# A recurrence on one core: the fourth head's decay levels move into the attention, a gate tile moves into the chunk steps, and the sample rows move ahead of a score block

## The chip, the cores and the metric

The kernel runs on one core of a Trainium2 chip. The metric is the device time of one launch in microseconds; of three timed runs before the change the median is 2238.07 us (2237.09 to 2239.33). Times inside the program are counted from the first instruction of one profiled execution. TensorE is called PE, VectorE DVE, ScalarE ACT, GpSimd POOL, and the engine that issues most transfers SP.

## The reference

One step of a decoder trunk of two layers, on 512 prompt tokens and 8 sequences of 8 sample tokens (576 columns in all). A layer projects its input, runs three mixers, merges them through sigmoid gates, and ends with a gated feed-forward block. The change lies in the second mixer, a gated recurrence with four heads:

```
def step(S, blk):                       # one chunk of one head
    qc, kc, vc, lc = blk
    L = jnp.cumsum(lc, axis=2)          # log decay since the chunk began
    inter = einsum('bhtk,bhkv->bhtv', qc * exp(L), S)
    diff = where(causal, L[:, :, :, None, :] - L[:, :, None, :, :], -inf)
    A = einsum('bhtk,bhsk,bhtsk->bhts', qc, kc, exp(diff))
    L_end = L[:, :, -1:, :]
    S = exp(L_end) * S + einsum('bhsk,bhsv->bhkv', kc * exp(L_end - L), vc)
    return S, inter + einsum('bhts,bhsv->bhtv', A, vc)
...
o_hg = rms_norm(o_hg) * silu(hgate)     # hgate: four 128-row tiles of x @ w_in
```

## The kernel before, in words

Every engine has an instruction order written out by hand; semaphores tie the engines together. In a layer come projections, the attention of the prompt (32 steps, a head and 128 queries each), the attention of the samples, the tiles of the pooling mixer and of `hgate`, the recurrence, the merge, the output projection and the feed-forward block.

The recurrence takes chunks of 128 tokens. A head has five steps: c = 0 to 3 for the prompt's chunks, c = 4 for the samples; step n of 20 is head n // 5, c = n % 5. exp(diff) is not formed per pair. A head has seven *levels* (block sizes 1 to 64): for each level a 512-column array holds log decays measured from the middle of a block (`level_differences`, L691 and L692), is put through exp by ACT (`decays_levels`, L1925), and its upper halves are multiplied by the queries (`level_scaled`, L700). The score block of a step is then many 32-column products on PE (`hg_pair_scores`, L1115 to L1124) and a transpose of the decayed keys (L1127). DVE masks and sums the score block (L2485, L2488, L2494); ACT copies the parts off the diagonal (`off_hg`, `hg_full`) and the transposed keys (`k_rows`), both at L1713. `hg_sums` on PE multiplies scores, state and values (L1152 to L1163), and DVE updates the state (L2516, L2518). In a sample step PE multiplies the eight sample states (the *sample rows*, L1173), makes the state updates (L1182) and the sample outputs (L1186, L1189); DVE copies the rows (`s_rows`, L2525) and updates the states (L2530).

The four heads have three level buffers; heads 0 and 3 share one. Head 2's levels are subtracted by POOL, head 3's too, at step 8 and after, when head 0's buffer is free. ACT makes head 3's exps in steps 10 and 11 (`LEVEL_STEPS`), DVE its products in steps 12 and 13 (`MULT_STEPS`).

Of `hgate`'s four tiles two are made whole on PE before the recurrence and put through silu by ACT. The other two are made inside it as four halves of 288 columns, one for each head, in pieces of 3, 3 and 2 matmuls (`gate_piece`, L1137) in the steps c = 1, 2, 3, between the next step's score block and this step's sums. ACT copies each half out of PSUM at c = 4 (`take_gate`) and applies silu in steps 13 and 19. PSUM bank 6 holds a half, and also sample state updates. exp and silu need different function tables on ACT; the table load before each change of function is an instruction of its own.

PE's loop over steps is:

```
for n in range(N_HG):
    if n + 1 < N_HG:
        hg_pair_scores(l, n + 1)
    h, c = divmod(n, N_CHUNK + 1)
    if 1 <= c < N_CHUNK:
        gate_piece(l, h, c - 1)
    hg_sums(l, n)
```

Of the kernel before, what the change touches and what calls it, by code (L numbers as in the profile page):

```python
# [71 lines left out]
LEV_BUF = (2, 0, 1, 2)  # L72
# [16 lines left out]
GATE_LOAD = MERGE0 - 1  # L89
# [54 lines left out]
TILE_YPOOL = TILE_HGATE + 2  # L144
# [21 lines left out]
def last_tiles():  # L166

    last = [TILE_CQ + 1, TILE_KPE, None, None, TILE_HQ + 1, TILE_HQ + 3, TILE_HI + 4, TILE_HI + 4]
    last += [TILE_U + 1, TILE_U + 3, TILE_HGATE + 1]
    assert len(last) == MERGE0 - 1  # L170
    return last
# [34 lines left out]
def build(nc, xT_in, w_stream, small_in, att_in, const_in, pages_in, kpe_in, page_table, pool_state,  # L206
          hgrn_state, conv_state, yT, ckv_out, kpe_out, pool_out, hgrn_p_out, hgrn_s_out, conv_out):
    with ExitStack() as ctx:
# [3 lines left out]
        def sem(name):  # L212
# [77 lines left out]
        lev_flat = [r1[:, 0:n_lev * SEQ], r1[:, n_lev * SEQ:2 * n_lev * SEQ], side[:, 4 * P + 2 * T:3 * HALF_DOWN]]  # L290
# [177 lines left out]
        def slot(tile):  # L468
            s = (tile + (TILE_U <= tile < TILE_YPOOL) + (TILE_YPOOL <= tile < TILE_SSQ_HG) + 3 * (tile >= TILE_SSQ_HG)) % 4
# [110 lines left out]
        gate_act = signal("gate_act", N_GATE + 2)  # L580
# [135 lines left out]
        def _(sp):  # L716
# [69 lines left out]
            with sp.Fori(0, DEPTH) as l:  # L786
# [53 lines left out]
                load(l, MERGE0)  # L840
# [65 lines left out]
        def _(pe):  # L906
# [222 lines left out]
            def gate_piece(l, h, x):  # L1129
                j, a = divmod(h, 2)  # L1130
                if h == 0 and x == 0:
                    pe.wait_ge(*w_ready[GATE_LOAD % 2].at(l, 16 * (GATE_LOAD // 2 + 1)))
                if h and x == 0:
                    pe.wait_ge(*hg_state.at(l, h * (N_CHUNK + 2)))
                w = w_tile(GATE_LOAD, j)
                for k in range(GATE_CHUNKS[x], GATE_CHUNKS[x + 1]):
                    mm = pe.matmul(bank[6][:, 0:HALF], w[k], xT[:, k, a * HALF:(a + 1) * HALF], start=(k == 0),  # L1137
                                   stop=(k == KD - 1))
                if x == 2:
                    mm.then_inc(gate_made.sem, 1)  # L1140

            def hg_sums(l, n):
# [22 lines left out]
                if h >= 1:  # L1165
                    pe.wait_ge(*hg_o_taken.at(l, 3 * h))
                    pe.wait_ge(*hg_sq.at(l, 2 * h))
                else:
                    pe.wait_ge(*state_s_ready.at(l, 16))
                for b in range(DEC_BATCH):  # L1170
                    x, j = divmod(b, S_PAIRS)
                    t0 = SEQ + min(DEC_SEQ * b, SAMPLES - SUB)
                    mm = pe.matmul(bank[5][SUB * j:SUB * (j + 1), 256 + x * P:256 + (x + 1) * P],  # L1173
                                   decayed[:, h % 2, 0, t0:t0 + SUB], state_s[:, b, h, :], start=True, stop=True)
                mm.then_inc(s_rows_made.sem, 1)
                pe.wait_ge(*gate_act.at(l, h + 1 + (h >= 2)))
# [351 lines left out]
            with pe.Fori(0, DEPTH) as l:  # L1528
# [170 lines left out]
        def _(act):  # L1699
# [94 lines left out]
            with act.Fori(0, DEPTH) as l:  # L1794
# [66 lines left out]
                for x in range(2):  # L1861
                    for lo, e in ((64, 0), (0, 1)):
                        rows = slice(lo, lo + 64)
                        copy(k96[rows, 2 * x:2 * x + 2, e, :], kpe[rows, 0:SEQ].unsqueeze(1).broadcast_to([64, 2, SEQ]),
                             scale=row_mask[rows, x:x + 1]).then_inc(k_rope.sem, 1)
                att_softmax(l, 0)
                for n in range(1, N_ATT + 2):
# [50 lines left out]
                def decays_levels(h, first, end):  # L1918
                    if first == 0:
                        act.wait_ge(*lev_diff.at(l, 2 * h + 1))  # L1920
                    b = LEV_BUF[h]
                    groups = [(first, end)] if b < 2 or end <= n_lev - 2 else [(v, v + 1) for v in range(first, end)]
                    for lo, hi in groups:
                        ap = lev_flat[b][:, lo * SEQ:hi * SEQ] if b < 2 or hi <= n_lev - 2 else level[b][lo]
                        ins = act.activation(ap, ap, ACT.Exp)  # L1925
                    if end == n_lev:
                        for ap in lev_s_flat[b]:
                            ins = act.activation(ap, ap, ACT.Exp)
                    if end == n_lev:
                        ins.then_inc(lev_exp.sem, 1)  # L1930
# [22 lines left out]
                for i, g in enumerate(GROUP_OF):  # L1953
                    act.wait_ge(*tile_ready.at(l, TILE_U + i + 1))
# [5 lines left out]
                decays_levels(1, 0, n_lev)  # L1960
                decays_ends(1)
                for j in range(2):
                    act.wait_ge(*tile_ready.at(l, TILE_HGATE + j + 1))
                    copy(two(hg_gate[:, j, :]), halves(TILE_HGATE + j), ACT.Silu).then_inc(tile_act.sem, 1)
# [10 lines left out]
                def gate_silu(j):  # L1975
                    act.wait_ge(*gate_act.at(l, (2, 5)[j - 2]))
                    act.activation(hg_gate[:, j, :], hg_gate[:, j, :], ACT.Silu).then_inc(gate_act.sem, 1)

                for n in range(N_HG):
# [22 lines left out]
                    if n == 13:  # L2002
                        gate_silu(2)
# [75 lines left out]
        def _(dve):  # L2079
# [173 lines left out]
            with dve.Fori(0, DEPTH) as l:  # L2253
# [170 lines left out]
                def ready_head(h):  # L2424
                    dve.wait_ge(*lev_exp.at(l, h + 1))
# [6 lines left out]
                dve.wait_ge(*log_k_ready.at(l, 1))  # L2432
                for h in range(2):
# [70 lines left out]
                def update(n):  # L2504
# [34 lines left out]
                for n in range(N_HG + 1):  # L2539
                    if n < N_HG:  # L2540
# [241 lines left out]
        def _(pool):  # L2782
# [146 lines left out]
            with pool.Fori(0, DEPTH) as l:  # L2929
# [26 lines left out]
                pool.tensor_tensor(log_k, log_k, logf, ALU.subtract).then_inc(log_k_ready.sem, 1)  # L2956

# [13 lines left out]
                differences(l, 3)  # L2971
# [311 lines left out]
```

## Time and profile before

| | |
|---|---|
| median of three timed runs | 2238.07 us |
| the profiled execution | 2238.98 us |
| its span, first to last instruction | 2237.2 us |
| mean granted clock of PE, as a share of 2.4 GHz | 0.993 |
| PE / DVE / POOL / ACT busy | 98% / 54% / 46% / 24% |

PE is busy nearly all the time; the other engines have room on average. The average hides single stretches in which another engine holds PE up; they are seen in the views of one stretch. A matmul of 32-bit floats stands in the trace as two records, so a gate piece of three matmuls reads x6. The recurrence of the first layer lies at 283 to 348 us, that of the second at 1392 to 1458 us.

### The profile page before, as it was taken

The page shows a single profiled execution, that of the slowest core. Times are in us where ns is not written, and L with a number is a line of the kernel's source. Part 1 is how long each engine was busy: PE and PEld are TensorE (multiplying, and loading weights), DVE is VectorE, ACT ScalarE, POOL GpSimd, SP SyncE. Part 2 cuts the span into 40 slices and gives each one's busy share as a digit, 9 for nine tenths or more (in the row PEclk, how much of TensorE's full clock was granted, in tenths as well). Part 3 has the DMA queues.
Part 4 walks back from the last instruction along what each step waited for, and adds up shares of the span by engine and source line. Part 5 has one row for each costly group of instructions (what it writes and reads, how often), then busy time and mean ns, then how long its engine had stood idle before and what let it go on. Part 6 is the DMA issues. An engine that isn't in the chain of part 4 may idle for free.

```text
span 2237.2 us, 37087 instructions
## 1 busy us (share of the span) xinstructions
PE 2189.7 (98%) x11824; PEld 1685.5 (75%) x11824; DVE 1202.1 (54%) x2152; ACT 525.9 (24%) x1112; POOL 1036.1 (46%) x1152
## 2 busy tenths in 40 slices
PE   8999999999999999999899999999999999999996
PEld 6776777777777777777676767777777777777775
DVE  2654675333577666661236447653336776666513
ACT  1453353111131111100134533521111411111002
POOL 3000146566656666633330002565767466665251
PEclk9999999999999999999999999999999999999998
DMA  5322113222132222122132221142211322222211
GB/s 210 106 74 78 43 64 134 67 85 85 57 108 77 85 82 75 69 74 77 39 135 88 75 68 66 41 144 81 79 68 57 127 75 75 75 78 79 86 52 42
DMA packets 51616, 183.54 MB, mean 82 GB/s; under 512 B 7234, under 2 KB 27970, under 8 KB 37762
## 3 DMA queue, kind: packets, MB, share of 16 engines
q1 hardware_dynamic: 50882, 178.49, 23.3%
q10 hardware_dynamic: 576, 3.06, 0.3%
q8 instruction: 84, 1.38, 0.3%
q14 instruction: 74, 0.61, 0.1%
HBM read 172.35 MB, written 9.18 MB: 81 GB/s over the span
## 4 chain that ended last, share of the span: by engine, by line
PE 93%; DVE 2%; issue 1%; POOL 1%; ACT 1%; SPq 1%; DMA 1%; DVEq 0%; ACTq 0%
PE ps L1315 25%; PE ps L1197 24%; PE ps L1357 17%; PE ps L917 9%; PE ps L986 3%; PE ps L949 2%; PE ps L1523 1%; PE ps L1387 1%; PE ps L1137 1%; PE ps L970 1%; PE ps L958 1%; PE ps L938 1%; PE ps L1038 1%; PE ps L1001 1%; PE ps L950 1%
## 5 line engine op out<-in xcount | busy, mean ns | idle before, releaser
L1315 PE MATMUL ps<-lq,mreg 128*128 128x288 f32 x1008 | 251.3, 406 | 0.0
L1315 PEld LDWEIGHTS ps<-lq,mreg 128*128 128x128 f32 x1008 | 191.5, 190 | 52.9
L1713 ACT ACTIVATE r<-ps 128x288 f32<-128x288 f32 (+7 forms) x264 | 112.9, 432 | 499.8 <-PE ps L1197 256.4
L1315 PE MATMUL ps<-xT,wring 128*128 128x288 f32 x672 | 169.8, 406 | 0.0
L917 PE MATMUL ps<-xT,wring 128*128 128x288 f32 (+2 forms) x640 | 156.2, 406 | 0.0
L1315 PEld LDWEIGHTS ps<-xT,wring 128*128 128x128 f32 x672 | 127.7, 190 | 35.3
L917 PEld LDWEIGHTS ps<-xT,wring 128*128 128x128 f32 x640 | 121.6, 190 | 33.7
L1197 PE MATMUL ps<-r,kbuf 128*128 128x288 f32 x576 | 143.6, 406 | 0.0
L1197 PEld LDWEIGHTS ps<-r,kbuf 128*128 128x128 f32 x576 | 109.4, 190 | 30.2
L2044 ACT ACTIVATE r<-r 128x592 f32<-128x592 f32 x44 | 30.7, 697 | 427.9 <-DVE r L2716 427.9
L2906 POOL TENSOR_TENSOR kbuf<-o_mla 128x288 f32<-128x288 f32 x42 | 33.4, 794 | 205.9 <-DVE o_mla L2680 205.9
L1713 ACT ACTIVATE o_mla<-ps 128x288 f32<-128x288 f32 (+1 forms) x108 | 45.2, 421 | 327.8 <-PE ps L1357 214.5
L2805 POOL TENSOR_TENSOR mreg<-vbuf,const 64x512 f32<-64x512 f32 x8 | 8.4, 1049 | 241.4 <-PE ps L1629 228.9
L1197 PE MATMUL ps<-xT,wring 128*128 128x288 f32 x448 | 113.4, 406 | 0.2 <-DMA wring<-w_stream 0.2
L2716 DVE SCALAR_TENSOR_TENSOR r<-r,small 128x592 f32<-128x592 f32 x88 | 106.3, 1209 | 12.4 <-DVE r L2713 12.1
L2713 DVE SCALAR_TENSOR_TENSOR r<-r,small 128x592 f32<-128x592 f32 x88 | 104.5, 1188 | 12.4 <-DVE r L2710 10.9
L1197 PEld LDWEIGHTS ps<-xT,wring 128*128 128x128 f32 x448 | 85.0, 190 | 24.5 <-issue 1.2
L1357 PE MATMUL ps<-r,side 128*128 128x288 f32 x372 | 92.7, 407 | 0.8 <-DVE r L2727 0.8
L1315 PE MATMUL ps<-xT,mreg 128*128 128x288 f32 x336 | 88.3, 406 | 0.0
L1315 PE MATMUL ps<-lq,wring 128*128 128x288 f32 x336 | 88.3, 406 | 0.0
L1197 PE MATMUL ps<-lq,r 128*128 128x288 f32 x336 | 87.4, 406 | 0.0
L1357 PEld LDWEIGHTS ps<-r,side 128*128 128x128 f32 x372 | 70.5, 190 | 21.0 <-issue 1.7
(459 smaller groups left out, 4659.4 us busy)
## 6 DMA issues: line engine op xcount, KB each, us to landing
wring<-w_stream SPq DMA_DIRECT2D x100, 1024.0 KB, 4.9
side<-w_stream SPq DMA_DIRECT2D x18, 704.0 KB, 4.5
r<-pages_in SPq DMA_DIRECT2D x80, 128.0 KB, 2.2
vbuf<-w_stream SPq DMA_DIRECT2D x12, 512.0 KB, 3.8
r<-w_stream SPq DMA_DIRECT2D x12, 512.0 KB, 3.6
wring<-w_stream SPq DMA_DIRECT2D x8, 704.0 KB, 4.1
r<-w_stream SPq DMA_DIRECT2D x6, 704.0 KB, 4.1
mreg<-pages_in SPq DMA_DIRECT2D x32, 128.0 KB, 2.1
```

What stands on the lines that cost most here:

```text
L917: mm = pe.matmul(out[0:w.shape[-1], a * 512:a * 512 + hi - lo], w, x[:, lo:hi], start=(k == 0), stop=(k == len(pairs) - 1))
L938: mm = pe.matmul(slot(tile + j)[:, a * 512:a * 512 + hi - lo], w, xT[:, k, lo:hi], start=(k == 0), stop=(k == KD - 1))
L949: pe.matmul(att_bank(n)[:, 0:keys], q96[:, j, e, t0:t0 + P], k96[:, j, e, 0:keys], start=True, stop=False)
L986: mm = pe.matmul(value_bank[g:g + rows, part * 256:(part + 1) * 256], xT[:, k, m * P:m * P + rows], w_slot[part][:, k * 256:(k + 1) * 256] ...
L1197: mm = pe.matmul(banks[name], ws[:, k * P:(k + 1) * P], xs[:, k, :], start=(k == 0), stop=(k == n - 1))
L1315: mm = pe.matmul(up_sum[name], ws[:, k * P:(k + 1) * P], xs[:, k, :], start=(k == 0), stop=(k == HK - 1))
L1357: mm = pe.matmul(res_bank(which, m, i - 1), ws[:, k * P:(k + 1) * P], x, start=(k == 0), stop=(k == len(xs) - 1))
L1713: return act.activation(out, in_, func, **more)
L2044: act.activation(conv_h[u][0][:, 0:CX - 2], conv_h[u][0][:, 0:CX - 2], ACT.Silu).then_inc(silu_done.sem, 1)
L2713: dve.scalar_tensor_tensor(out=out, in0=src[:, 1:CX - 1], scalar=scalar(col + 2 * KF), in1=out, op0=ALU.mult, op1=ALU.add).then_inc(conv_s ...
L2716: dve.scalar_tensor_tensor(out=out, in0=src[:, 2:CX], scalar=scalar(col + 4 * KF), in1=out, op0=ALU.mult, op1=ALU.add).then_inc(conv_done. ...
L2906: pool.tensor_tensor(up_v[u], up_u2[u], up_p5s[u], ALU.add).then_inc(up_v_ready.sem, 1)
```

## The change

The levels of head 3 get a buffer of their own, `own_lev` (room comes from a smaller reserve for descriptors of POOL's transfers; POOL issues none here). POOL subtracts them right after `log_k`, ACT makes one exp after each even attention step from 12 to 24, and POOL multiplies by the queries. Steps 10 to 13 of the recurrence lose this work.

One of the two whole `hgate` tiles is no longer made before the recurrence. Its two halves join the other four: six halves of eight matmuls, in pieces of 4 in all steps c = 0 to 3 of heads 0 and 1, and of 2 in heads 2 and 3; at c = 0 the piece stands behind the sums. ACT takes the halves in steps 1, 3, 6, 8, 13 and 18 and applies silu in steps 7, 9 and 18. The pooling products wait for the silu of the one tile left (before: for the tile four back).

In a sample step PE's sample rows stand ahead of the next head's score block, and DVE's copy of them ahead of its work on that block. ACT makes head 1's levels and decays between the second and the third tile of the pooling input. SP's first load of merge weights waits for the second gate half.

```
-LEVEL_STEPS = {3: (2, 0, 3), 5: (2, 3, 7), 10: (3, 0, 3), 11: (3, 3, 7)}
+LEVEL_STEPS = {3: (2, 0, 3), 5: (2, 3, 7)}
+EARLY_LEVELS = {12 + 2 * v: v for v in range(7)}
-MULT_STEPS = {6: (2, 0, 2), 7: (2, 2, 4), 8: (2, 4, 7), 12: (3, 0, 3), 13: (3, 3, 7)}
-N_GATE = 4
-GATE_CHUNKS = (0, 3, 6, 8)
+MULT_STEPS = {6: (2, 0, 2), 7: (2, 2, 4), 8: (2, 4, 7)}
+N_GATE = 6
+GATE_PIECES = ((4, 4, 4, 4), (4, 4, 4, 4), (2, 2, 2, 2), (2, 2, 2, 2))
+GATE_TAKES = {1: 0, 3: 1, 6: 2, 8: 3, 13: 4, 18: 5}
+GATE_SILU = {7: 1, 9: 2, 18: 3}
...
-                load(l, MERGE0)
+                sp.wait_ge(*tile_ready.at(l, LAST_TILE[MERGE0 - 2] + 1))
+                sp.wait_ge(*gate_made.at(l, 2))
+                load_after(l, MERGE0, LOAD)
...
                 for i, g in enumerate(GROUP_OF):
-                    pe.wait_ge(*taken_at(l, TILE_YPOOL + i - 4))
+                    pe.wait_ge(*taken_at(l, TILE_YPOOL - 1))
...
                 for n in range(N_HG):
+                    h, c = divmod(n, N_CHUNK + 1)
+                    if c == N_CHUNK:
+                        hg_rows(l, h)
                     if n + 1 < N_HG:
                         hg_pair_scores(l, n + 1)
-                    h, c = divmod(n, N_CHUNK + 1)
                     if 1 <= c < N_CHUNK:
-                        gate_piece(l, h, c - 1)
+                        gate_pieces(l, h, c)
                     hg_sums(l, n)
+                    if c == 0:
+                        gate_pieces(l, h, c)
...
+                    if n in EARLY_LEVELS:
+                        decays_levels(HEADS - 1, EARLY_LEVELS[n], EARLY_LEVELS[n] + 1)
...
                     copy(k_rows[0:w, n % 2, :], turned_bank(n)[0:w, :]).then_inc(hg_k_rows.sem, 1)
+                    if n in GATE_TAKES:
+                        take_gate(GATE_TAKES[n])
                     if c == N_CHUNK:
-                        take_gate(h)
-                        if h == 3:
-                            gate_silu(3)
...
-                    if n == 13:
-                        gate_silu(2)
+                    if n in GATE_SILU:
+                        gate_silu(GATE_SILU[n])
...
                 for n in range(N_HG + 1):
+                    if n and n % (N_CHUNK + 1) == 0:
+                        dve.wait_ge(*s_rows_made.at(l, n // (N_CHUNK + 1)))
+                        dve.tensor_copy(s_rows, bank[5][:, 256:512]).then_inc(hg_o_taken.sem, 1)
                     if n < N_HG:
                         pair_sums(n)
...
+                pool.wait_ge(*log_k_ready.at(l, 1))
+                differences(l, HEADS - 1)
+                pool.wait_ge(*tile_act.at(l, taken(TILE_HQ + 3)))
+                pool.wait_ge(*lev_exp.at(l, 1))
+                level_scaled(pool, HEADS - 1).then_inc(late_ready.sem, 1)
```

Three places show the new order. First ACT in step 3, before the change and then after it; 128x288 is a gate half, 128x1536 the first exp of head 2's levels, `mreg<-ps` the copy of transposed keys, with 64 rows that of step 4.

```order
L1713 ACTIVATE mreg<-ps 128x128
L1925 ACT_TABLE_LOAD
L1925 ACTIVATE r<-r 128x1536
L1982 REGISTER_ALU
L1984 REGISTER_ALU
L1713 ACTIVATE mreg<-ps 64x128
L1713 ACTIVATE r<-ps 128x288
```

```order
L1738 ACTIVATE mreg<-ps 128x128
L1995 REGISTER_ALU
L1738 ACTIVATE r<-ps 128x288
L1898 ACT_TABLE_LOAD
L1898 ACTIVATE r<-r 128x1536
L2009 REGISTER_ALU
L2011 REGISTER_ALU
L1738 ACTIVATE mreg<-ps 64x128
```

The table load and the exp, which stood ahead of any gate half, stand behind the copy of the second half.

Then ACT at the end of the last head, steps 18 and 19, before and after; 128x576 is the silu of the last gate tile.

```order
L1713 ACTIVATE off_hg<-ps 32x32 x2
L1713 ACTIVATE mreg<-ps 128x128
L1982 REGISTER_ALU
L1984 REGISTER_ALU
L1713 ACTIVATE mreg<-ps 64x128
L1713 ACTIVATE r<-ps 128x288
L1976 REGISTER_ALU
L1977 ACTIVATE r<-r 128x576
L1996 REGISTER_ALU
L1997 ACTIVATE lq<-ps 128x512
```

```order
L1738 ACTIVATE mreg<-ps 128x128
L1995 REGISTER_ALU
L1738 ACTIVATE r<-ps 128x288
L2003 REGISTER_ALU
L2004 ACT_TABLE_LOAD
L2004 ACTIVATE r<-r 128x576
L2009 REGISTER_ALU
L2011 REGISTER_ALU
L1738 ACTIVATE mreg<-ps 64x128
L2022 REGISTER_ALU
L2023 ACTIVATE lq<-ps 128x512
```

The half and the silu stand one copy earlier, and a table load stands between them.

Last PE at the end of a head (the sample step of head 1), before and after; 32x128 are the sample rows, 32x32 the score block.

```order
L1163 MATMUL ps<-vbuf,mreg 128x128
L1115 MATMUL ps<-lq,r 32x32 x4
L1115 MATMUL ps<-r 32x32 x20
L1119 MATMUL ps<-r 32x64 x2
L1124 MATMUL ps<-r 32x32 x2
L1127 MATMUL ps<-const,mreg 128x128
L1173 MATMUL ps<-r,mreg 32x128 x8
```

```order
L1195 MATMUL ps<-vbuf,mreg 128x128
L1163 REGISTER_ALU
L1164 REGISTER_ALU
L1170 MATMUL ps<-r,mreg 32x128 x8
L1126 MATMUL ps<-lq,r 32x32 x4
L1126 MATMUL ps<-r 32x32 x20
L1130 MATMUL ps<-r 32x64 x2
L1135 MATMUL ps<-r 32x32 x2
L1138 MATMUL ps<-const,mreg 128x128
```

The rows stand ahead of the score block instead of behind it.

## Rows read from the trace of the kernel before

**Rows 1.** The page's first part: busy time, share, instructions of the engines.

```profile
PE 2189.7 (98%) x11824; PEld 1685.5 (75%) x11824; DVE 1202.1 (54%) x2152; ACT 525.9 (24%) x1112; POOL 1036.1 (46%) x1152
```

**Rows 2.** Stretches: length, busy PE, PEld, DVE, ACT, POOL, granted clock, DMA.

```profile
320.00:325.00 5.00, 4.35 (x68) 3.59 (x67) 4.50 (x15) 4.96 (x15) 0.27 (x1) 0.53 0.02 3
325.00:330.00 5.00, 5.00 (x39) 4.06 (x39) 2.36 (x8) 3.91 (x12) 1.40 (x1) 0.78 0.00 2
...
345.00:350.00 5.00, 4.21 (x34) 2.80 (x34) 3.78 (x12) 2.37 (x4) 5.00 (x4) 1.00 0.60 210
...
1430.00:1435.00 5.00, 4.92 (x68) 4.06 (x69) 4.18 (x15) 4.96 (x19) 0.27 (x1) 0.50 0.02 3
```

**Rows 3.** Timeline around step 10: start, length, instruction, idle before and its releaser.

```profile
287.46 1.62 PE L1137 MATMUL ps<-xT,wring 128*128 128x288 f32 x6
...
317.68 1.48 ACT L1925 ACTIVATE side<-side 128x1536 f32<-128x1536 f32 x1 [5.50 <-POOL mreg L692]
...
319.70 0.49 PE L1152 MATMUL ps<-off_hg,vbuf 128*128 128x128 f32 x2 [1.75 <-ACT off_hg L1713]
...
320.84 0.80 PE L1154 MATMUL ps<-mreg,vbuf 128*128 128x128 f32 x2 [0.65 <-DVE mreg L2494]
...
323.79 3.09 PE L1137 MATMUL ps<-xT,wring 128*128 128x288 f32 x6
```

**Rows 4.** Waits of the whole program: total us, times, longest.

```profile
PEld ps L1186 <- DVE r L2525: 7.8, 8, 1.2
...
PE ps L1186 <- DVE r L2525: 1.1, 4, 0.4
...
PE ps L1115 <- issue: 0.9, 2, 0.6
```

**Rows 5.** Timeline at the end of the last head, first layer.

```profile
344.00 0.38 PE L1152 MATMUL ps<-off_hg,vbuf 128*128 128x128 f32 x2
344.20 0.41 ACT L1713 ACTIVATE r<-ps 128x288 f32<-128x288 f32 x1 [0.62 <-PE ps L1137]
...
344.64 0.68 ACT L1977 ACTIVATE r<-r 128x576 f32<-128x576 f32 x1
...
344.99 0.64 PE L1173 MATMUL ps<-r,mreg 128*32 128x128 f32 x16
345.36 0.75 DVE L2500 SCALAR_TENSOR_TENSOR r<-ps,small,r 128x512 f32<-128x512 f32 x1 [1.24 <-ACT r L1977]
...
346.42 1.13 PE L1182 MATMUL ps<-mreg 32*128 32x512 f32 x4 [0.79 <-DVE side L2518]
```

**Rows 6.** Timeline of steps 3 and 4, ACT and PE.

```profile
291.85 1.28 ACT L1925 ACT_TABLE_LOAD   x1
293.14 1.48 ACT L1925 ACTIVATE r<-r 128x1536 f32<-128x1536 f32 x1
...
294.53 0.26 ACT L1713 ACTIVATE mreg<-ps 64x128 f32<-64x128 f32 x1
...
295.67 0.27 PE L1115 MATMUL ps<-lq,r 128*32 128x32 f32 x8
...
296.62 0.65 PE L1173 MATMUL ps<-r,mreg 128*32 128x128 f32 x16
```

**Rows 7.** Timeline ahead of the recurrence: pooling products, silu, pooling input.

```profile
279.36 4.05 PE L917 MATMUL ps<-r,small 128*128 128x288 f32 x16
...
279.56 0.65 ACT L1713 ACTIVATE r<-ps 128x576 f32<-128x576 f32 x1 [6.86 <-PE ps L917]
...
273.25 0.22 DVE L2461 SCALAR_TENSOR_TENSOR r<-r 128x64 f32<-128x64 f32 x1
```

**Rows 8.** Timeline in and after the attention: POOL, and one ACT copy.

```profile
117.14 5.05 POOL L2956 TENSOR_TENSOR kbuf<-kbuf,lq 128x2304 f32<-128x2304 f32 x1 [60.88 <-DVE side L2341]
236.63 1.09 POOL L2805 TENSOR_TENSOR mreg<-vbuf,const 64x512 f32<-64x512 f32 x1 [114.44 <-PE ps L1629]
...
165.74 0.60 ACT L1713 ACTIVATE r<-ps 128x512 f32<-128x512 f32 x1 [0.93 <-PE ps L958]
```

More of the change, by code:

```diff
@@ L143 @@
 TILE_HGATE = TILE_U + 4
-TILE_YPOOL = TILE_HGATE + 2
+TILE_YPOOL = TILE_HGATE + 1
 GROUP_OF = (3, 2, 1, 0)
@@ L168, in last_tiles @@
     last = [TILE_CQ + 1, TILE_KPE, None, None, TILE_HQ + 1, TILE_HQ + 3, TILE_HI + 4, TILE_HI + 4]
-    last += [TILE_U + 1, TILE_U + 3, TILE_HGATE + 1]
+    last += [TILE_U + 1, TILE_U + 3, TILE_HGATE]
     assert len(last) == MERGE0 - 1
@@ L293, in build @@
         level += [[lev_flat[2][:, v * SEQ:(v + 1) * SEQ] for v in range(n_lev - 2)] + [lev_c, lev_spare[:, 0:SEQ]]]
-        s_cols = SMALL_LEVELS * SAMPLES
+        level += [[own_lev[:, v * SEQ:(v + 1) * SEQ] for v in range(n_lev)]]
         o = 2 * n_lev * SEQ + N_DIAG * SUB + 4096
         lev_s_flat = [[lev_s[:, 0:s_cols]], [lev_s[:, s_cols:s_cols + SAMPLES], lev_spare[:, SEQ + s_cols:], r1[:, o:o + SAMPLES]],
-                      [lev_spare[:, SEQ:SEQ + s_cols]]]
+                      [lev_spare[:, SEQ:SEQ + s_cols]], [own_lev[:, n_lev * SEQ:]]]
         level_s = [[ap[:, i:i + SAMPLES] for ap in aps for i in range(0, ap.shape[1], SAMPLES)] for aps in lev_s_flat]
@@ L468, in slot @@
         def slot(tile):
-            s = (tile + (TILE_U <= tile < TILE_YPOOL) + (TILE_YPOOL <= tile < TILE_SSQ_HG) + 3 * (tile >= TILE_SSQ_HG)) % 4
+            s = (tile + (TILE_U <= tile < TILE_YPOOL) + 2 * (TILE_YPOOL <= tile < TILE_SSQ_HG)) % 4
             if tile in (TILE_SSQ_CKV, TILE_SSQ_CQ):
@@ L579, in build @@
         gate_made = signal("gate_made", N_GATE)
-        gate_act = signal("gate_act", N_GATE + 2)
+        gate_act = signal("gate_act", N_GATE + 3)
         s_rows_made = signal("s_rows_made", HEADS)
@@ L1127, in hg_pair_scores, with gate_acts @@
                 pe.transpose(turned_bank(n)[0:w, :], decayed[:, h % 2, 1, t0:t0 + w], ident).then_inc(hg_turned.sem, 1)
[L1129 to L1140, printed above, removed]
+            def gate_acts(before):
+                return before + sum(t < GATE_STEP_OF[before - 1] for t in GATE_SILU) if before else 0
@@ new lines, in gate_pieces @@
+            def gate_pieces(l, h, c):
+                first = 8 * (2 * h if h < 2 else h + 2) + sum(GATE_PIECES[h][:c])
+                for piece in range(first, first + GATE_PIECES[h][c]):
+                    half, k = divmod(piece, KD)
+                    j, a = divmod(half + 2, 2)
+                    n = GATE_LOAD + j // 2
+                    if piece == 0 or (k == 0 and j == 2):
+                        pe.wait_ge(*w_ready[n % 2].at(l, 16 * (n // 2 + 1)))
+                    if k == 0:
+                        pe.wait_ge(*hg_state.at(l, h * (N_CHUNK + 2)))
+                        pe.wait_ge(*gate_act.at(l, gate_acts(half)))
+                    mm = pe.matmul(bank[6][:, 0:HALF], w_tile(n, j % 2)[k], xT[:, k, a * HALF:(a + 1) * HALF],
+                                   start=(k == 0), stop=(k == KD - 1))
+                    if k == KD - 1:
+                        mm.then_inc(gate_made.sem, 1)
@@ new lines, in hg_rows @@
+            def hg_rows(l, h):
+                if h >= 1:
+                    pe.wait_ge(*hg_o_taken.at(l, 3 * h))
+                    pe.wait_ge(*hg_sq.at(l, 2 * h))
+                else:
+                    pe.wait_ge(*state_s_ready.at(l, 16))
+                for b in range(DEC_BATCH):
+                    x, j = divmod(b, S_PAIRS)
+                    t0 = SEQ + min(DEC_SEQ * b, SAMPLES - SUB)
+                    mm = pe.matmul(bank[5][SUB * j:SUB * (j + 1), 256 + x * P:256 + (x + 1) * P],
+                                   decayed[:, h % 2, 0, t0:t0 + SUB], state_s[:, b, h, :], start=True, stop=True)
+                mm.then_inc(s_rows_made.sem, 1)
@@ L1164, in hg_sums @@
                     return
[L1165 to L1176, printed above, removed]
+                pe.wait_ge(*gate_act.at(l, gate_acts((2, 4, 5, 6)[h])))
                 pe.wait_ge(*hg_k_rows.at(l, n + 1))
@@ L1865, in _, with decays_levels @@
                              scale=row_mask[rows, x:x + 1]).then_inc(k_rope.sem, 1)
+                def decays_levels(h, first, end):
+                    if first == 0:
+                        act.wait_ge(*lev_diff.at(l, LEV_DIFFS[h]))
+                    b = LEV_BUF[h]
+                    groups = [(first, end)] if b != 2 or end <= n_lev - 2 else [(v, v + 1) for v in range(first, end)]
+                    for lo, hi in groups:
+                        ap = lev_flat[b][:, lo * SEQ:hi * SEQ] if b != 2 or hi <= n_lev - 2 else level[b][lo]
+                        ins = act.activation(ap, ap, ACT.Exp)
+                    if end == n_lev:
+                        for ap in lev_s_flat[b]:
+                            ins = act.activation(ap, ap, ACT.Exp)
+                    if end == n_lev:
+                        ins.then_inc(lev_exp.sem, 1)
                 att_softmax(l, 0)
@@ L1916, in _ @@
                 smp_take_cols(S_PAIRS - 1)
[L1918 to L1930, printed above, removed]
                 def decays_ends(h):
-                    act.wait_ge(*lev_diff.at(l, 2 * h + 2))
+                    act.wait_ge(*lev_diff.at(l, END_DIFFS[h]))
                     act.activation(k_now[h % 2], k_now[h % 2], ACT.Exp)
@@ L1953, in _ @@
                 for i, g in enumerate(GROUP_OF):
+                    if i == 2:
+                        decays_levels(1, 0, n_lev)
+                        decays_ends(1)
                     act.wait_ge(*tile_ready.at(l, TILE_U + i + 1))
@@ L1959, in _ @@
                          ).then_inc(tile_act.sem, 1)
[L1960 to L1964, printed above, removed]
+                act.wait_ge(*tile_ready.at(l, TILE_HGATE + 1))
+                copy(two(hg_gate[:, 0, :]), halves(TILE_HGATE), ACT.Silu).then_inc(tile_act.sem, 1)
                 def take_gate(half):
@@ L1968, in take_gate @@
                     act.wait_ge(*gate_made.at(l, half + 1))
-                    copy(hg_gate[:, 2 + j, a * HALF:(a + 1) * HALF], bank[6][:, 0:HALF]).then_inc(gate_act.sem, 1)
+                    copy(hg_gate[:, 1 + j, a * HALF:(a + 1) * HALF], bank[6][:, 0:HALF]).then_inc(gate_act.sem, 1)
                 def sample_square(h):
@@ L2510, in update @@
                         dve.wait_ge(*hg_o.at(l, 2 * h + 1))
-                        dve.wait_ge(*(taken_at(l, TILE_HGATE + h) if h < 2 else gate_act.at(l, 3 * h - 3)))
+                        dve.wait_ge(*(gate_act.at(l, (4, 6, 9)[h - 1]) if h else taken_at(l, TILE_HGATE)))
                         gated(h, 0, SEQ, bank[4])
```

29 lines of the change are left out of this document (17 added, 12 removed).

## The prediction

> **What bounds the kernel now.** I read the shares of the engines first. PE is busy 98% of the span, the next engine 54% [rows 1], so work added to DVE, ACT or POOL costs nothing where PE doesn't wait for it. Work moved within PE changes nothing by itself. What can change the time is PE's idle stretches and its clock, which I then looked for in the stretches of the recurrence, the only stage where the diff touches PE's waits. The reader is to see two things there.
>
> The first is step 10. POOL ends head 3's differences late; ACT stands 5.50 us until they come and starts the exp at 317.68; the scores behind it are late, and PE idles 1.75 us until 319.70 and 0.65 more until 320.84, for DVE [rows 3]. That is 2.4 us of idle in under 3.
>
> The second follows it. The granted clock is 0.53 from 320 to 325 and 0.78 from 325 to 330, and 0.50 in the same place of the second layer [rows 2]: PE runs at 1.2 instead of 2.4 GHz for a while. A gate piece of three matmuls takes 3.09 us there and 1.62 before [rows 3]. At half speed were (1 - 0.53) / 0.5 x 5 = 4.7 us and (1 - 0.78) / 0.5 x 5 = 2.2 us, 6.9 us together. Half of that is lost, 3.45, less half of the 0.65 us in which PE idled anyway: 3.1 us. So step 10 costs a layer 2.4 us of idle and about 3.15 of clock (3.1 to 3.2).
>
> **The change, part by part.** All sums are per layer; there are two. The profiled execution took 2238.98 us, 0.91 over the median; I work with differences and set them on the median, 2238.07.
>
> Levels of head 3. ACT's exps and POOL's differences leave step 10, so both idles go, -2.40; what is late next there is nothing that I find, since DVE loses its ten products of steps 12 and 13 too. The new place is the attention. POOL subtracts when log_k's operation of 117.14 us (5.05 long) is done and has nothing to do until 236.63 (114.44 us idle) [rows 8], so its subtractions and multiplications are hidden. ACT's seven exps, of about one 512-column copy each (0.60), stand where such a copy had 0.93 us of idle before it [rows 8]: hidden, 0. If every one were exposed it would be 7 x 0.60 = 4.2.
>
> Gate matmuls. The sixteen that move take the same time in or before the recurrence: 0.
>
> Pooling products. They now wait for the silu of the only whole hgate tile. Before, they began at 279.36 and the silu, 0.65 long, at 279.56 [rows 7]. So they begin 0.20 + 0.65 + 0.06 for the signal later, +0.9. Their other input, ready at 273.25 [rows 7], doesn't count. Bounds: 0 to +0.9; I take the end, as nothing else of PE's stands there.
>
> Sample rows. PE waited for DVE's copy of them 1.1 us over four of eight heads, 0.55 a layer; its weight loads waited 7.8 over eight, 3.9 a layer, half of which at most could count [rows 4]. So 0 to -2.5; I take -0.8, near the row of PE itself. The two issue pauses before a score block, 0.9 together [rows 4], should shrink with four gate matmuls ahead of them: -0.3 (0 to -0.45).
>
> Step 3. ACT's table load and exp of head 2 (1.28 + 1.48) stood ahead of the key copy of step 4 [rows 6], without a gate half. Now the take of the second half stands ahead of all three, and it can't begin before PE has ended that half. From there ACT needs 0.20 to start and 0.41 for the take (as at the end of head 3 [rows 5]), 1.28, about 1.4 for the exp and 0.26 for the key copy, 3.6 with the signal. PE has step 3's sums (0.99, from 344.00 to 344.99 [rows 5]), the rows (0.65) and the score block (0.95) [rows 6] to do before its state update needs the keys: 2.5. So PE waits about +1.2 at the end of head 0. Bounds: 0, if ACT is ahead of this, and +3.6, if nothing covers it.
>
> End of head 3. The half comes out of PSUM at 344.20, silu follows at 344.64 with no table load, and PE waits 0.79 for the state update at 346.42 [rows 5]. Now the last exps lie behind the silu of step 9's, so a table load of 1.28 [rows 6] stands between take and silu; DVE's gated state work waits for the silu (1.24 idle, released by it [rows 5]). The whole load lands on PE: +1.29, idle 0.79 + 1.29 = 2.1. Nothing hides it; bounds 0 to +2.0, the load and an exp's rest of 0.7. Two smaller waits in heads 2 and 3, whose pieces shrink from three matmuls to two: +0.1. The load of merge weights that SP now issues later is wanted only after the last head: 0.
>
> Sum without the clock: -2.40 + 0.9 - 0.8 - 0.3 + 1.2 + 1.3 + 0.1 = 0.0. What is left is the clock: -3.15 for the fall of step 10, and +3.15 if a new idle stretch brings a fall of its own. An idle of 0.79 was not followed by one (the row from 345 to 350 has 1.00), 2.4 us in two parts was [rows 2, 3]; the new 2.1 lies between, nearer to the upper.
>
> On the table loads the row shows 291.85 + 1.28 = 293.13, and the exp starts at 293.14 [rows 6]: a switch costs its load and no more. The Trainium skill ("ScalarE: Activation LUTs", section "What ACT_TABLE_LOAD costs") adds a drain of about 1.38 us to each switch, 2.66 in all. By that rule the two exposed loads would bring 2 x 1.38 more a layer, 5.5 in all; the trace speaks against it, and I hold it for 0.02.
>
> **Rivals.**
> 1. Neither layer's clock falls at the end of head 3: 2 x -3.15 = -6.3, 2231.8 us. For it: the longest idle there is one of 2.1 and the clock stood through 0.79. Against: nearer to 2.4. 0.31.
> 2. It falls in both: 0.0 x 2, 2238.1 us. 0.17.
> 3. Slower: the wait at the end of head 0, which no row of before has, is nearer 2 us than 1.2 and drops the clock there in both layers, besides both falls at the end of head 3. 2 x 3.15 on top of rival 2: 2244.4. It decides where that idle passes what the clock stood through, between 0.79 and 2.4; for it, ACT's queue at step 3 is 3.6 us long [rows 6]; against, 1.2 is nearer to 0.79. 0.08.
> 4. The attention doesn't hide the new exps or POOL's operations: 4.2 a layer, 8.4 in all on the forecast, 2243.3. Against: the idle of both engines [rows 8]. 0.04.
> 5. The change doesn't do what it says: some other late input still holds step 10, and the fall stays, +3.15 a layer on rival 2 or on the forecast, some 2241. 0.04.
>
> **How the numbers follow.** Forecast: the clock falls again in one of the two layers, at even chances a layer: -3.15, 2234.9 us, chance 0.34. With rivals 1 to 5 (0.31, 0.17, 0.08, 0.04, 0.04) and 0.02 for the longer switch (about 2240 to 2244) that is 1. A measurement of this kernel can tell about 0.2% from no change, 4.5 us: faster is under 2233.6, slower over 2242.5. The terms carry some 2 us of error (bounds above), so 0.13 of the forecast's 0.34 and 0.29 of the first rival's 0.31 and 0.02 of the second's lie under 2233.6: faster 0.44. Of the third rival 0.06, of the fourth 0.03 and of the rest 0.02 lie over 2242.5: slower 0.11. Same 0.45. The range from 2230 to 2241 leaves out the third and fourth and the lower edge of the first; the likeliest case's own range is 2233 to 2237.
>
> **What would show it.** Step 10: an exp without wait and a granted clock of 1.00 from 315 to 330. Ahead of the recurrence: the products about 0.9 us after the silu's turn. End of head 0: idle of about 1.2 before the first state update, released by the key copy. End of head 3: a table load of 1.28 between take and silu, 2.1 of idle, and a clock row under 1.00 in one layer behind it. Wrong would be: step 10 still idle; an idle at the end of head 0 of 2 us or more with a fall; PE waiting in the attention for ACT's copies.

## The result and the profile after

The changed kernel takes 2246.32 us (median of six runs, 2239.83 to 2249.55), the kernel before 2237.66 beside it: a ratio of 1.0036 (95% interval 1.0026 to 1.0046). The forecast was 2234.9 with a range of 2230 to 2241. It is wrong in sign and outside the range. A second set of eight runs gave 2243.89 against 2237.70, ratio 1.0027 (1.0017 to 1.0037). The runs of the changed kernel spread over 8 to 10 us, those of before over 2 to 5 (one run of before in the second set, 3343.42 us at a mean clock of 0.642, is left out of this spread). The profiled run of after is the shortest of its six, 2239.83, so its trace alone can't explain the median; the profiles of the experiments below are needed for that.

The page of after, engines' busy time, share and instructions:

```profile
PE 2190.0 (98%) x11824; PEld 1685.1 (75%) x11824; DVE 1205.0 (54%) x2132; ACT 531.5 (24%) x1124; POOL 1045.6 (47%) x1172
```

The shares are those of [rows 1]. Now the stretches of after that answer to [rows 2] (length, busy PE, PEld, DVE, ACT, POOL, granted clock, DMA):

```profile
295.00:300.00 5.00, 5.00 (x75) 3.94 (x74) 3.58 (x13) 3.85 (x14) 2.68 (x3) 0.66 0.11 43
315.00:320.00 5.00, 5.00 (x133) 3.96 (x132) 4.08 (x15) 1.25 (x6) 2.68 (x3) 1.00 0.01 3
320.00:325.00 5.00, 5.00 (x98) 4.27 (x97) 2.73 (x8) 4.86 (x16) 0.17 (x1) 1.00 0.01 3
325.00:330.00 5.00, 5.00 (x94) 3.68 (x94) 3.76 (x12) 2.52 (x11) 1.54 (x2) 1.00 0.01 2
340.00:345.00 5.00, 2.86 (x28) 1.94 (x29) 1.81 (x5) 3.13 (x5) 4.92 (x5) 0.89 0.60 210
345.00:350.00 5.00, 5.00 (x15) 3.20 (x12) 2.35 (x9) 1.64 (x3) 2.07 (x1) 0.50 0.25 105
...
1430.00:1435.00 5.00, 5.00 (x99) 4.31 (x98) 2.54 (x9) 4.93 (x15) 0.80 (x1) 1.00 0.02 3
1450.00:1455.00 5.00, 2.86 (x27) 1.43 (x25) 1.43 (x3) 3.02 (x5) 4.92 (x5) 0.83 0.56 210
1455.00:1460.00 5.00, 5.00 (x15) 3.56 (x14) 2.35 (x9) 2.25 (x3) 1.46 (x1) 0.50 0.37 154
```

Step 10 is clean: full clock and a busy PE from 315 to 330, and at 1430. But the clock is now down in two other places: behind the end of head 0 of the first layer, where 0.66 is (1 - 0.66) / 0.5 x 5 = 3.4 us at half speed or 1.7 lost, and behind the end of head 3 (0.50 in both layers). The timeline of after at these two places (start, length, instruction, idle before and its releaser), first the end of head 0:

```profile
291.26 0.41 ACT L1738 ACTIVATE r<-ps 128x288 f32<-128x288 f32 x1 [4.51 <-PE ps L1156]
291.69 1.28 ACT L1898 ACT_TABLE_LOAD   x1
292.98 1.48 ACT L1898 ACTIVATE r<-r 128x1536 f32<-128x1536 f32 x1
294.37 0.25 ACT L1738 ACTIVATE mreg<-ps 64x128 f32<-64x128 f32 x1
...
294.75 1.13 PE L1203 MATMUL ps<-mreg 32*128 32x512 f32 x4 [1.23 <-ACT mreg L1738]
```

ACT stands idle for 4.51 us, takes the half, and only then loads the table for exps that could have run in that idle time; PE waits 1.23 us for the key copy behind them. Then the end of head 3:

```profile
340.50 0.41 ACT L1738 ACTIVATE r<-ps 128x288 f32<-128x288 f32 x1 [2.57 <-PE ps L1156]
340.93 1.28 ACT L2004 ACT_TABLE_LOAD   x1
342.23 0.68 ACT L2004 ACTIVATE r<-r 128x576 f32<-128x576 f32 x1
...
343.01 0.75 DVE L2527 SCALAR_TENSOR_TENSOR r<-ps,small,r 128x512 f32<-128x512 f32 x1 [2.60 <-ACT r L2004]
...
344.07 2.08 PE L1203 MATMUL ps<-mreg 32*128 32x512 f32 x4 [2.14 <-DVE side L2545]
```

The idle is 2.14, where [rows 5] had 0.79, and the four state updates behind it take 2.08 instead of 1.13 us: they run at 1.2 GHz (the granted clock is 0.50 there). Ahead of the recurrence PE waits for the silu, as foreseen:

```profile
271.54 0.65 ACT L1738 ACTIVATE r<-ps 128x576 f32<-128x576 f32 x1 [5.74 <-PE ps L928]
...
272.25 2.94 PE L928 MATMUL ps<-r,small 128*128 128x288 f32 x11 [0.74 <-ACT r L1738]
```

### The profile page after: what moved, and what is told of

It is laid out like the page before. It is cut to its first block, busy times and chain, and to the rows that moved or that the text cites. A ratio compares the mean times of both kernels' runs of the same rounds, so it can differ in the third digit from the quotient of the medians.

```text
span 2238.0 us, 37129 instructions
## 1 busy us (share of the span) xinstructions
PE 2190.0 (98%) x11824; PEld 1685.1 (75%) x11824; DVE 1205.0 (54%) x2132; ACT 531.5 (24%) x1124; POOL 1045.6 (47%) x1172
## 4 chain that ended last, share of the span: by engine, by line
PE 95%; DVE 2%; issue 1%; ACT 1%; SPq 1%; DMA 1%; ACTq 0%; DVEq 0%
PE ps L1336 25%; PE ps L1218 24%; PE ps L1378 17%; PE ps L928 8%; PE ps L997 3%; PE ps L1156 2%; PE ps L960 2%; PE ps L1544 1%; PE ps L1408 1%; PE ps L981 1%; PE ps L1126 1%; PE ps L969 1%; PE ps L949 1%; PE ps L1049 1%; PE ps L1012 1%
## 5 line engine op out<-in xcount | busy, mean ns | idle before, releaser
L1738 ACT ACTIVATE r<-ps 128x288 f32<-128x288 f32 (+8 forms) x266 | 113.2, 430 | 510.5 <-PE ps L1218 255.9
L1336 PEld LDWEIGHTS ps<-xT,wring 128*128 128x128 f32 x672 | 127.7, 190 | 35.3
L928 PE MATMUL ps<-xT,wring 128*128 128x288 f32 (+2 forms) x576 | 140.7, 406 | 0.0
L928 PEld LDWEIGHTS ps<-xT,wring 128*128 128x128 f32 x576 | 109.4, 190 | 30.3
L1218 PEld LDWEIGHTS ps<-xT,wring 128*128 128x128 f32 x448 | 85.0, 190 | 25.7 <-issue 2.4
L2848 POOL TENSOR_TENSOR kbuf<-kbuf,xT 128x576 f32<-128x576 f32 x20 | 28.2, 1409 | 118.4 <-DVE xT L2211 118.4
```

The costliest lines, as they stand in the source:

```text
L928: mm = pe.matmul(out[0:w.shape[-1], a * 512:a * 512 + hi - lo], w, x[:, lo:hi], start=(k == 0), stop=(k == len(pairs) - 1))
L1218: mm = pe.matmul(banks[name], ws[:, k * P:(k + 1) * P], xs[:, k, :], start=(k == 0), stop=(k == n - 1))
L1336: mm = pe.matmul(up_sum[name], ws[:, k * P:(k + 1) * P], xs[:, k, :], start=(k == 0), stop=(k == HK - 1))
L1738: return act.activation(out, in_, func, **more)
```

## The experiments

**1. The changed kernel again** (`after_again`), no edit.

> The changed kernel unchanged. Theory A (clock): PE's idle at the end of head 0 (1.2 to 1.5 us) drops the granted clock in most runs, for longer than the 3.4 us of the profiled one, and the idle at the end of head 3 (2.3 us) drops it in all; times 2240 to 2250, and the longer a run, the lower its mean granted clock (0.992 down to 0.990). Theory B: the weight load at the start of the second layer is issued late by a chance that differs from run to run; times spread alike, but the clock doesn't follow them, and the profile shows an idle other than 1.6 us at about 1146 us.

Measured: 2243.89 us, 2240.69 to 2248.33, mean clock 0.990 to 0.993; the two longest runs (2245.60 and 2248.33) have the 0.990. Two points of theory A missed: the fall at the end of head 0 is again 3.4 us long, not longer, and in the second layer neither idle is followed by one. This profile (a run of 2244.92) shows what neither theory named. It has a stall in the attention, in both layers. The timeline of the first:

```profile
128.94 0.65 POOL L700 TENSOR_TENSOR own_lev<-lq 128x256 f32<-128x256 f32 x1
...
129.23 3.37 DVE L2189 TENSOR_SCALAR r<-r,stat 128x128 f32<-128x128 f32 x1
...
129.54 0.64 POOL L701 TENSOR_TENSOR own_lev<-kbuf,lq 128x256 f32<-128x256 f32 x1
...
130.14 0.63 POOL L700 TENSOR_TENSOR own_lev<-lq 128x256 f32<-128x256 f32 x1
...
130.73 0.63 POOL L701 TENSOR_TENSOR own_lev<-kbuf,lq 128x256 f32<-128x256 f32 x1
...
131.32 0.62 POOL L700 TENSOR_TENSOR own_lev<-lq 128x256 f32<-128x256 f32 x1
...
131.90 0.62 POOL L701 TENSOR_TENSOR own_lev<-kbuf,lq 128x256 f32<-128x256 f32 x1
...
132.66 0.33 PE L969 MATMUL ps<-const,r 128*128 128x128 f32 x1 [1.74 <-DVE r L2189]
```

DVE's first normalisation of the attention, which multiplies 128 probabilities a row by one number, starts inside one of POOL's new subtractions and ends at 132.60, just behind the last of them, which ends at 132.52. It takes 3.37 us; before the change it took 0.29:

```profile
129.19 0.29 DVE L2163 TENSOR_SCALAR r<-r,stat 128x128 f32<-128x128 f32 x1
```

PE waits 1.74 us for it, and its clock falls for a while behind that (stretches of the changed kernel's profile):

```profile
130.00:135.00 5.00, 2.99 (x15) 1.55 (x13) 3.89 (x5) 1.66 (x5) 2.52 (x5) 0.82 0.31 90
135.00:140.00 5.00, 5.00 (x26) 2.93 (x25) 1.71 (x6) 2.56 (x7) 0.00 (x0) 0.84 0.32 86
```

In the first profile of after the same operation got through behind one subtraction (it ends at 129.38, that subtraction at 129.30), although it began as far into it (0.29 us):

```profile
128.65 0.65 POOL L700 TENSOR_TENSOR own_lev<-lq 128x256 f32<-128x256 f32 x1
...
128.94 0.44 DVE L2189 TENSOR_SCALAR r<-r,stat 128x128 f32<-128x128 f32 x1
```

So a layer is hit (the normalisation held until POOL's row is over) or not, from run to run. Theory B found little: PE does wait longer for weights at the start of the second layer in both profiles of after (1.39 and 1.52 us, 0.22 before), but no clock fall follows, and the two differ by little. The wait in before and in the first profile of after:

```profile
1145.85 3.42 PE L1197 MATMUL ps<-xT,wring 128*128 128x288 f32 x13 [0.22 <-DMA wring<-w_stream]
...
1147.28 2.93 PE L1218 MATMUL ps<-xT,wring 128*128 128x288 f32 x11 [1.39 <-DMA wring<-w_stream]
```

**2. The exps of step 3 ahead of the take** (`levels_first`).

```
+ if n in LEVEL_STEPS: decays_levels(*LEVEL_STEPS[n])
  if n in GATE_TAKES: take_gate(GATE_TAKES[n])
- if n in LEVEL_STEPS: decays_levels(*LEVEL_STEPS[n])   # stood behind the square
```

> In step 3 ACT makes head 2's exps ahead of the take of the gate half. Theory A: the idle of 1.45 at the end of head 0 goes in both layers (-2.9) and its clock falls too (-3 to -7): 2236 to 2240, spread under 3 us; the falls at the end of head 3 stay. Theory B: -2.9 only, about 2243, spread as before.

Measured: 2238.24 (2233.95 to 2244.61), 5.7 less than after in the same session. The idle at the end of head 0 and its clock falls are gone (stretch 295 to 300: 1.00). The median fits theory A; the spread of 10.7 us doesn't. One layer of its profile was hit in the attention.

**3. Half of the last silu early** (`silu_half`), which also takes the table load out of the end.

```
+ if n == 17: act.activation(hg_gate[:, 3, 0:HALF], hg_gate[:, 3, 0:HALF], ACT.Silu)
  # gate_silu(3) in step 18 then does the other half only
```

> Half of head 3's silu, and with it the table load, moves to step 17. Theory A: the idle at the end of head 3 shrinks from 2.3 to about 1.0 (-2.7 for two layers) and its two clock falls go (-6.8): about 2237, with the spread that the falls at the end of head 0 leave. Theory B: -2.7 only, about 2243.5.

Measured: 2237.35 (2232.38 to 2240.70), 6.5 less than after. The idle at the end of head 3 is 0.62, and no clock fall follows in either layer. Both layers of its profile had the stall in the attention, and both the fall at the end of head 0.

**4. Both edits** (`both_fixes`).

> Both edits together. Theory A: no clock fall in either recurrence, 2227 to 2231, spread under 3 us, mean clock 0.994 to 0.995. Theory B: -5.6, about 2240.5, spread as before.

Measured: 2231.29 (2225.49 to 2234.81), ratio to before 0.9971 (0.9960 to 0.9982). No clock fall in either recurrence; theory A holds for the recurrence, theory B (2240.5) is out. The median is 0.3 over theory A's range, and a spread of 9 us remained where under 3 was expected, and the profile had both layers hit. Where the spread comes from was now the question.

**5. POOL's row of subtractions broken up** (`paced`): the last two levels wait for DVE's first two normalisations.

```
- differences(l, HEADS - 1)
+ level_differences(pool, HEADS - 1, 0, n_lev - 2)
+ for v in (1, 2):
+     pool.wait_ge(*att_probs.at(l, v))
+     ins = level_differences(pool, HEADS - 1, n_lev - 3 + v, n_lev - 2 + v)
+ ins.then_inc(lev_diff.sem, 1)
```

> The changed kernel, but POOL subtracts head 3's last two levels one after each of DVE's first two normalisations of the attention. Theory P: POOL's unbroken row of subtractions holds DVE's normalisation (3.37 instead of 0.29 us), so PE idles 1.9 us and its clock falls, 3.6 us for each layer that is hit; paced, no normalisation is longer than 0.6 us, no idle of PE stands at 130 and 1240, and the median comes to 2238 to 2242, spread under 5. Theory Q: the long normalisation has another cause (its own waits): it stays, 2242 to 2249.

Measured: 2240.24 (2235.59 to 2241.18, nine of eleven runs between 2239.4 and 2241.2), 3.7 less than `after_again`, which is from another session. No stall of PE at 130 or 1240. Two points of the expectation missed: the spread is 5.6 us, not under 5, and a normalisation of 1.02 us is in the profile, since POOL's row still covers its start, but now it ends with that row and PE isn't waiting yet. The timeline:

```profile
129.42 1.02 DVE L2189 TENSOR_SCALAR r<-r,stat 128x128 f32<-128x128 f32 x1
...
129.72 0.64 POOL L701 TENSOR_TENSOR own_lev<-kbuf,lq 128x256 f32<-128x256 f32 x1
130.52 0.63 POOL L700 TENSOR_TENSOR own_lev<-lq 128x256 f32<-128x256 f32 x1 [0.16 <-DVE r L2189]
```

**6. A shorter row** (`short_row`): as 5, but only the last level (1.25 us) waits, for the first normalisation.

> The changed kernel, only the last level's subtractions of head 3 (1.25 us) waiting for the first normalisation, so that POOL's unbroken row ends at about 131.3 instead of 132.5. Theory P: in a layer that is hit the normalisation lasts from 129.2 until the row ends, 2.1 to 2.2 us instead of 3.37, and PE idles 0.6 to 0.8 instead of 1.9 us. Theory Q: 3.37 as before, or 0.3.

Measured: 2241.60 (2240.08 to 2244.55). The first layer was hit, the second not. The timeline has the length that theory P foretold (PE's idle of 0.58 is just under its 0.6 to 0.8):

```profile
128.91 2.21 DVE L2189 TENSOR_SCALAR r<-r,stat 128x128 f32<-128x128 f32 x1
...
130.39 0.65 POOL L701 TENSOR_TENSOR own_lev<-kbuf,lq 128x256 f32<-128x256 f32 x1
...
131.18 0.33 PE L969 MATMUL ps<-const,r 128*128 128x128 f32 x1 [0.58 <-DVE r L2189]
```

The subtractions before the wait end at 131.04, the normalisation at 131.12. A row 1.25 us shorter made it 1.16 us shorter. That DVE's operation is held until POOL's unbroken row ends is shown. The Trainium skill ("SBUF — State Buffer", section "Who interferes with whom") says that GpSimd and a DVE operation of this kind (a `tensor_scalar`, in a mode that takes both ports) exclude each other: whoever issues first holds the shared ports for the whole instruction, and the other is blocked. The traces agree that one blocks the other, but only in a part of the layers is it for one instruction. In the eleven profiles with the new subtractions the normalisation started inside one of them in all 22 layers, and each time it ended 0.08 to 0.09 us behind the end of a subtraction: in 8 layers the one it had met, in 14 the last of the row (with one, three or five more behind the one it had met), and in none one between. What decides between the two is open.

**7. The levels alone** (`levels_only`): the kernel before with a buffer for head 3's levels and their work in the attention, all else as it was.

> The kernel before with nothing but head 3's levels moved into the attention. Prediction's terms: both idles of step 10 and both clock falls go, 2 x (2.4 + 3.15) = 11.1 from 2237.7, so 2226.6 without a hit. Theory P: each hit layer gives 3.6 back: 2227 to 2234, in steps. Theory Q: 2226.6, spread under 3.

Measured: 2231.45 (2227.67 to 2238.41), ratio 0.9975 (0.9964 to 0.9986). The clock at step 10 stays full:

```profile
312.00:317.00 5.00, 4.88 (x134) 4.23 (x134) 4.67 (x17) 2.13 (x10) 2.67 (x3) 1.00 0.01 3
317.00:322.00 5.00, 5.00 (x98) 4.34 (x97) 2.07 (x7) 4.87 (x15) 1.40 (x1) 1.00 0.02 3
322.00:327.00 5.00, 4.51 (x90) 3.01 (x89) 3.44 (x11) 1.92 (x7) 0.49 (x1) 1.00 0.01 2
```

The lowest run, 2227.67, is 10 below before (expected 11.1); one layer of the profile was hit. The highest, 2238.41, is above the range of theory P, and the runs don't stand in clear steps.

**8. The levels alone, paced** (`levels_only_paced`), 7 with the edit of 5.

> The same with the last two levels paced. Theory P: 2226 to 2229, spread under 4, no long normalisation. Theory Q: as levels_only.

Measured: 2229.09 (2227.22 to 2230.42), ratio 0.9958 (0.9944 to 0.9971), a spread of 3 us and no stall in the attention. It is as theory P has it, but for a normalisation of 1.02 us as in 5, and 11 us below `paced`: that is what the other parts of the change cost as they were made. Its profile, of the longest run (2230.42), has one fall, at the end of head 3 in the second layer, behind the idle of 0.79 that no fall followed in the profile of before:

```profile
1445.45 1.13 PE L1188 MATMUL ps<-mreg 32*128 32x512 f32 x4 [0.79 <-DVE side L2527]
```

```profile
1445.00:1450.00 5.00, 4.55 (x16) 3.00 (x17) 3.17 (x12) 2.53 (x4) 4.81 (x3) 0.74 0.61 247
```

**9. The best version** (`best`): the changed kernel with edits 2, 3 and 5, and the first two pooling products waiting only for the tile whose PSUM they take.

```
- pe.wait_ge(*taken_at(l, TILE_YPOOL - 1))
+ pe.wait_ge(*taken_at(l, TILE_YPOOL + min(i - 3, -1)))
```

> The changed kernel with both edits to ACT, the pacing, and the first two pooling products waiting only for the tiles whose PSUM they take. Theory P: the lowest run of both_fixes (2225.5) less 0.9 per layer of pooling wait: 2223 to 2226, spread under 3. Theory Q: 2229 to 2232, spread as in both_fixes.

Measured: 2224.97 (2223.47 to 2225.85), ratio to before 0.9941 (0.9928 to 0.9955): faster than both kernels, in every run, and 4.1 below `levels_only_paced`, so the other parts gain once their waits are gone. Its page, and its timeline at the two ends:

```profile
PE 2182.4 (98%) x11824; PEld 1680.6 (76%) x11824; DVE 1203.1 (54%) x2132; ACT 532.2 (24%) x1126; POOL 1046.3 (47%) x1172
```

```profile
286.24 1.28 ACT L1898 ACT_TABLE_LOAD   x1
287.54 1.48 ACT L1898 ACTIVATE r<-r 128x1536 f32<-128x1536 f32 x1
290.73 0.41 ACT L1738 ACTIVATE r<-ps 128x288 f32<-128x288 f32 x1 [1.71 <-PE ps L1156]
...
337.41 0.41 ACT L1738 ACTIVATE r<-ps 128x288 f32<-128x288 f32 x1 [2.57 <-PE ps L1156]
337.85 0.44 ACT L2005 ACTIVATE r<-r 128x288 f32<-128x288 f32 x1
...
339.46 1.13 PE L1203 MATMUL ps<-mreg 32*128 32x512 f32 x4 [0.62 <-DVE side L2548]
```

The load and the exp lie in ACT's idle time ahead of the take; between take and silu there is no load; PE's updates take 1.13 again. PE's busy time is 7.6 us less than after's for the same 11824 matmuls. That fits the clock: in the two recurrences PE stood at half of it for 17.1 us in after (8.5 lost) and not at all here.

**10. The sample rows back behind the score block** (`rows_back`), else `best`.

> The best kernel with the sample rows, and DVE's copy of them, behind the next head's score block again, as before the change. If the prediction's term is right (0.8 a layer, or 1.1 by the stretches that went): 1.6 to 2.3 slower than best, 2226.5 to 2227.5, with PE idle before the sample outputs in three heads. Rival: the rows' order is worth nothing, since the copy was late only behind other waits: 2225, no idle there.

Measured: 2225.99 (2225.96 to 2228.60) against 2224.97, from different sessions whose runs of before differ by 0.2 (2237.71 and 2237.52): about 1 us slower, so the order is worth something, some 0.5 a layer, less than the 0.8 to 1.1 expected. The waits of [rows 4] are back: that of the weight loads in the first recurrence, and PE's own in the whole program, 0.9 us in two waits, one in each layer, where one in each of three heads was expected:

```profile
PEld ps L1207 <- DVE r L2572: 3.9, 4, 1.3
...
PE ps L1207 <- DVE r L2572: 0.9, 2, 0.5
```

## Why the prediction was wrong

Step by step, per layer.

- Step 10. Right: the two idles (-2.4) and the fall are gone in every profile, and by `levels_only_paced`, whose profile has a fall elsewhere, the move alone is worth 8.4 us of the 11.1 that were worked out for two layers.
- Pooling products. Right: 0.74 of idle, 0.9 predicted.
- Wait at the end of head 0. Right in size: 1.23, 1.2 predicted. A part of that is luck: the prediction's own terms, 3.6 less 0.99 + 0.65 + 0.95, make 1.0.
- End of head 3. Right in size: 2.14 of idle, 2.1 predicted; the table load of 1.28 is nearly the whole of the difference, 1.35. The load and the next operation follow each other without the drain that the prediction weighed, here too (340.93 + 1.28 = 342.21, silu at 342.23).
- Sample rows and issue pauses. From the start of the state updates to that of the sample outputs PE took 1.24, 1.34 and 1.47 us in heads 0 to 2 of the first layer before, 1.05 to 1.06 after: 0.9 less a layer, 0.8 predicted (`rows_back` was expected from 1.1, which the traces don't show). Taken back alone, the order costs about 0.5. The two issue pauses are gone: 0.45 a layer, 0.3 predicted.

So the waits came to -2.40 + 0.74 + 1.23 + 1.35 - 0.9 - 0.45 = -0.4 a layer, where 0.0 was summed: this part of the sum held. Two steps failed. The table has what they rest on, from all profiles of changed kernels: the first normalisation of the attention, PE's idle at the two ends (none where no idle is left), and behind each how long the granted clock was 0.50, all in us, first and second layer.

| profile | normalisation, layers 1 and 2 | half clock behind it | idle, end of head 0 | half clock | idle, end of head 3 | half clock |
|---|---|---|---|---|---|---|
| after | 0.44, 0.43 | 0, 0 | 1.23 | 3.4, 0 | 2.14 | 6.8, 6.8 |
| `after_again` | 3.37, 3.39 | 3.4, 3.4 | 1.23 | 3.4, 0 | 2.14 | 6.8, 0 |
| `levels_first` | 3.36, 0.43 | 3.4, 0 | none | 0, 0 | 2.14 | 3.4, 3.4 |
| `silu_half` | 3.35, 3.36 | 0, 3.4 | 1.23 | 3.4, 3.4 | 0.62 | 0, 0 |
| `both_fixes` | 3.35, 3.36 | 3.4, 3.4 | none | 0, 0 | 0.62 | 0, 0 |
| `levels_only` | 0.43, 3.35 | 0, 0 | none | 0, 0 | 0.79 | 0, 0 |
| `short_row` | 2.21, 0.43 | 0, 0 | 1.23 | 0, 3.4 | 2.14 | 6.8, 6.8 |
| `paced` | 1.02, 1.02 | 0, 0 | 1.23 | 3.4, 3.4 | 2.14 | 6.8, 6.8 |
| `levels_only_paced` | 1.02, 0.42 | 0, 0 | none | 0, 0 | 0.79 | 0, 3.4 |
| `best` | 0.43, 0.43 | 0, 0 | none | 0, 0 | 0.62 | 0, 0 |
| `rows_back` | 1.04, 1.03 | 0, 0 | none | 0, 0 | 0.62 | 0, 0 |

First, the step that chose the forecast, that the clock falls again in one of two layers. The idle of 2.14 was followed by a fall in nine of ten places (five profiles with it, two layers each: after, `after_again`, `levels_first`, `paced`, `short_row`), as long as the one of step 10 in seven of them. And the idle of 1.23 at the end of head 0 was followed by one in seven of ten (after, `after_again`, `silu_half`, `paced`, `short_row`), half as long each time, costing 1.7 instead of the 3.15 of rival 3. That rival had the mechanism, though it asked for an idle nearer 2 us, and was given 0.08; that its 2244.4 lies close to the measured times is in part luck, since it holds no term for the attention.

Second, the step that put the work in the attention at 0 because POOL and ACT had been idle there. Its instructions were hidden on their own engines; the price was on a third one. In six profiles with the unbroken row, 8 of 12 layers were hit; a hit costs 1.7 us of PE and in six of eight a clock fall of 1.7. Rival 4 had the place, but looked for its price in ACT's queue, and set 0.04 by the idle of both engines. Nothing in the prediction asked what DVE does while POOL runs.

Put together, for two layers: waits -0.9; the falls of step 10 -6.3; at the end of head 3 +5.1 (2 x (7 x 3.15 + 2 x 1.7) / 10); at the end of head 0 +2.4 (0.7 x 2 x 1.7); hits +4.0 (2 x 0.67 x (1.7 + 0.75 x 1.7)); the late weight load of the second layer +1.2. That is +5.5, where +8.7 and +6.2 were measured; the shares are those of the profiles, and what made up the rest, 0.7 to 3.2 us, isn't shown. In the first set the five runs without a profile have mean clocks of 0.990 and 0.991, the profiled one 0.992, so they spent more time at half speed. Four of these terms were undone by an edit and went (2, 3, 5, 9); the clock's share of each was not taken apart from its idle by a run of its own.

Open: why SP issues that weight load late in some profiles (some 1.2 us in after; PE waits 1.71 us there in `best`) and not in others; no edit touched it.

## What to carry to other kernels

An idle engine is not free room: before work is put on POOL, list the DVE operations that will run beside it, look for one whose duration changes, and don't issue a long unbroken row of instructions across an operation that PE waits for. A gain that consists of a clock fall taken away can be lost again by an idle of one or two microseconds that the same edit opens elsewhere, so look at every new wait for what it does to the clock, not only for its length. Where runs spread more than before, one profile is one draw: take several, and compare durations of the same instruction between them.

## What the runs showed of the hardware that was not expected

- A row of back-to-back POOL instructions can hold a DVE operation until the whole row is over (3.37 and 2.21 us for 0.29 of work), and whether it does is not decided by when the operation starts: 0.29 us into a subtraction, it took 0.44 once and 3.37 another time. A row of POOL multiplies, later in the attention, never held the same operation for a row (0.41 at most in all profiles), but there it starts 0.53 us or more into a multiply, so this is no like comparison.
- A fall after idle was not a matter of its length alone: the stall of 1.7 us in the attention was followed by one in six of eight cases, the wait of 1.2 to 1.7 us for weights at the start of the second layer in none of six, and the idle of 0.6 to 0.8 at the end of head 3 in one of fourteen.
